# A matrix inverse by doubling: block transposes on VectorE, and narrow tiles for the upper levels

## The reference

```python
lower = jnp.where(strict, jnp.einsum('bhncd,bhnsd->bhncs', kb, k) * decay, 0.0)
tinv = lax.linalg.triangular_solve(lower + eye, eye, left_side=True, lower=True, unit_diagonal=True)
u = jnp.einsum('bhncs,bhnsv->bhncv', tinv, v * beta)
w = jnp.einsum('bhncs,bhnsd->bhncd', tinv, kb * jnp.exp(g))
```

## Time and profile before

| | us |
|---|---|
| median of 3 runs | 1895.49 (1892.24 to 1897.36) |
| the profiled execution, its time | 1895.78 |
| its span, first to last instruction | 1893.8 |
| PE busy | 1811.6 (96%) |
| DVE busy | 1004.5 (53%) |
| ACT busy | 645.8 (34%) |
| POOL busy | 558.5 (29%) |

### The profile page before, as it was taken

One profiled execution on the slowest core, in us unless ns is written; L12 is line 12 of the kernel. 1 busy time (PEld: TensorE's weight loads), 2 busy tenths in 40 slices (PEclk: granted clock), 3 DMA queues, 4 the chain that ended last, 5 costly groups with the idle time before them and its releaser, 6 DMA issues.

```text
span 1893.8 us, 29921 instructions
## 1 busy us (share of the span) xinstructions
PE 1811.6 (96%) x11609; PEld 1743.1 (92%) x11609; DVE 1004.5 (53%) x971; ACT 645.8 (34%) x1028; POOL 558.5 (29%) x492
## 2 busy tenths in 40 slices
PE   5999999987999999999996999999999999999997
PEld 5999999987999999999996989899999999999996
DVE  4477777762445445535545055645554554454556
ACT  6443333354344344335333253221222112122123
POOL 2344555423442333333240211121222212213120
PEclk9999999998999999999998999999999999999999
DMA  6132332323232422422338411111111111111112
GB/s 180 48 95 86 90 91 86 87 107 115 69 92 73 114 61 59 113 61 71 104 95 252 156 34 34 34 56 44 48 52 43 45 44 55 44 33 55 44 44 89
DMA packets 189848, 146.99 MB, mean 78 GB/s; under 512 B 22940, under 2 KB 178115, under 8 KB 188660
## 3 DMA queue, kind: packets, MB, share of 16 engines
q1 hardware_dynamic: 148740, 114.88, 20.8%
q10 hardware_dynamic: 40848, 31.49, 5.4%
q0 software_dynamic: 224, 0.12, 0.0%
HBM read 109.72 MB, written 36.74 MB: 77 GB/s over the span
## 4 chain that ended last, share of the span: by engine, by line
PE 83%; DVE 5%; issue 5%; DMA 2%; ACT 2%; POOLq 1%; DVEq 1%; POOL 1%; SPq 1%; ACTq 0%
PE gb L707 57%; PE db L970 12%; PE db L812 7%; PE db L809 3%; PE db L748 1%; DMA yo<-ot_d 1%; PE db L849 1%; PE db L848 1%; DVEq L1346 1%; DVE hx L1613 1%; POOLq L653 0%; PE db L923 0%; DVE fino L1719 0%; PE db L720 0%; ACT hx L1016 0%
## 5 line engine op out<-in xcount | busy, mean ns | idle before, releaser
L707 PE MATMUL gb<-u_hi,w_hi 128*128 128x342 f32 (+2 forms) x2520 | 827.1, 328 | 17.6 <-ACT ht L1255 7.3
L707 PE MATMUL gb<-u_lo,w_hi 128*128 128x342 f32 (+2 forms) x2520 | 812.2, 322 | 0.0
L707 PE MATMUL gb<-u_hi,w_lo 128*128 128x342 f32 (+2 forms) x2520 | 809.0, 321 | 0.0
L595 POOL TENSOR_TENSOR w_lo<-w_raw,w_hi 128x1024 fp32r<-128x1024 f32 x128 | 335.8, 2630 | 884.6 <-ACT w_hi L1012 884.6
L707 PEld LDWEIGHTS gb<-u_hi,w_hi 128*128 128x128 f32 x2520 | 479.9, 190 | 19.6 <-issue 18.0
L707 PEld LDWEIGHTS gb<-u_lo,w_hi 128*128 128x128 f32 x2520 | 480.0, 190 | 0.5
L707 PEld LDWEIGHTS gb<-u_hi,w_lo 128*128 128x128 f32 x2520 | 479.1, 190 | 0.0
L1390 DVE SCALAR_TENSOR_TENSOR cacc<-xb,prm,cacc 128x1040 f32<-128x1040 f32 x72 | 174.3, 2421 | 11.2 <-issue 10.5
L1685 DVE TENSOR_TENSOR h<-h,db 128x512 f32<-128x512 f32 x176 | 117.1, 685 | 57.4 <-PE db L970 57.0
L970 PE MATMUL db<-w_hi,a_hi 128*128 128x512 f32 x352 | 140.2, 398 | 3.4 <-DVE a_lo L1709 2.9
L1012 ACT ACTIVATE w_hi<-w_raw 128x1024 fp32r<-128x1024 f32 x128 | 133.6, 1052 | 18.7 <-ACT tm L1077 17.3
(11 more groups left out here) (218 smaller groups left out, 2104.7 us busy)
## 6 DMA issues: line engine op xcount, KB each, us to landing
w_raw<-in_w_in SPq DMA_DIRECT2D x53, 512.0 KB, 3.9
w_raw<-in_w_up SPq DMA_DIRECT2D x44, 512.0 KB, 3.7
qkv_d<-tm ACTq DMA_DIRECT2D x24, 576.0 KB, 3.1
tk<-qkv_d SPq DMA_DIRECT2D x9, 1536.0 KB, 7.7
w_raw<-in_w_down SPq DMA_DIRECT2D x22, 512.0 KB, 3.3
ot_d<-ots ACTq DMA_DIRECT2D x9, 512.0 KB, 3.2
yb_d<-ybs ACTq DMA_DIRECT2D x8, 513.0 KB, 3.8
yl<-yb_d SPq DMA_DIRECT2D x8, 513.0 KB, 5.2
```

The lines of the kernel that those rows point to most:

```text
L595: pool.tensor_tensor(w_lo[:, n % SLOTS, :], w_raw[:, n % SLOTS, :], w_hi[:, n % SLOTS, :].bitcast(F32), ALU.subtract).then_inc(s_wlo, 1)
L707: mm = pe.matmul(gb[:, bank, 0:w], wt, u, start=(k == 0 and m == 0), stop=(k == KT - 1 and m == 2))
```

## The change

- The transposes TT0, T0 and T1 leave PE and ACT. DVE makes rr out of bd, and tt_m out of rr after Y0, by an instruction that transposes each 32x32 block in its place. Both matrices have nothing outside their 32x32 diagonal blocks then.
- Level 32 computes only the tiles that it needs. X1 is two products for each head with 32 weight columns and 32 moving columns; Y1 is three, of which the third makes the lower tile for tt_m. DVE evicts tiles of 32 partitions, two or three instructions for each half.
- Level 64 (the top) is one quarter: X2 and Y2 are products of 64 by 64 columns.
- STEPS has 19 steps. The pieces are dealt out anew: GROW has 1 and not 3, OT 5 and not 2, Y0 2 and not 1, X1 1 and not 0; TT0, T0 and T1 had one each.
- In the projection stage ACT squares the transposed tile out of db, and only for the 16 tiles of q and k. POOL only makes w_lo there. DVE sums only those 16 tiles, and the last sum leaves the pooling part.

```diff
-STEPS = ["P1", "TKN", "V", "TKB", "GROW", "KK", "TQ", "TKG", "O", "SU", "QK", "TQD", "OT", "TT0"]
+STEPS = ["P1", "TKN", "V", "TKB", "GROW", "KK", "TQ", "TKG", "O", "SU", "QK", "TQD", "OT"]
...
-    DOUBLING += [f"X{_n}", f"Y{_n}"] + ([f"T{_n}"] if _n < len(LEVELS) - 1 else [])
+    DOUBLING += [f"X{_n}", f"Y{_n}"]
...
-FILLS = {"P1": 2, "TKN": 0, "V": 1, "TKB": 0, "GROW": 3, "KK": 2, "TQ": 2, "TKG": 2, "O": 2, "SU": 2, "QK": 1,
-         "TQD": 1, "OT": 2, "TT0": 1, "X0": 1, "Y0": 1, "T0": 1, "X1": 0, "Y1": 1, "T1": 1, "X2": 0, "Y2": 1}
+FILLS = {"P1": 2, "TKN": 0, "V": 1, "TKB": 0, "GROW": 1, "KK": 2, "TQ": 2, "TKG": 2, "O": 2, "SU": 2, "QK": 1,
+         "TQD": 1, "OT": 5, "X0": 1, "Y0": 2, "X1": 1, "Y1": 1, "X2": 0, "Y2": 1}
...
@@ gpsimd
-                pool.tensor_tensor(sq[:, :, :], tm[:, :, :], tm[:, :, :], ALU.mult).then_inc(s_sq, 1)
...
@@ tensor
+                elif name == "X1":
+                    def left_squares(o, m):
+                        for z in (0, HALF):
+                            t = pe.matmul(o[z + SQ:z + HALF, 0:SQ], at_m[:, m, z + SQ:z + HALF], tt_m[:, m, z:z + SQ],
+                                          start=True, stop=True)
+                        return t
+                    each([(s_tt, 2 * (c - 1))], left_squares)
+                elif name == "Y1":
+                    def right_squares(o, m):
+                        for z in (0, HALF):
+                            pe.matmul(o[z:z + SQ, 0:SQ], nmx[:, m, z:z + SQ], rr[:, m, z + SQ:z + HALF],
+                                      start=True, stop=True)
+                        return pe.matmul(o[SQ:HALF, 0:SQ], rr[:, m, SQ:HALF], nmx[:, m, 0:SQ], start=True, stop=True)
+                    each([done["X1"], done["Y0"]], right_squares)
+                elif name == TOP_X:
+                    each([done["Y1"]], lambda o, m: pe.matmul(
+                        o[HALF:, 0:HALF], at_m[:, m, HALF:], tt_m[:, m, 0:HALF], start=True, stop=True))
+                elif name == LAST_Y:
+                    each([done[TOP_X]], lambda o, m: pe.matmul(
+                        o[0:HALF, 0:HALF], nmx[:, m, 0:HALF], rr[:, m, HALF:], start=True, stop=True))
...
@@ scalar
+                    if squared:
+                        q = act.activation(sq[:, c0:c1, :].rearrange("p c d -> p (c d)"), db[:, r, 0:(c1 - c0) * P],
+                                           ACT.Square)
...
@@ vector
+            def turned_squares(dst, src):
+                return dve.transpose(dst.rearrange("p m c -> p (m c)"), src.rearrange("p m c -> p (m c)"))
...
+                elif name == "X0":
+                    dve.wait_ge(s_bd, 16 + 16 * BLKS * c)
+                    dve.wait_ge(s_ps["V"], 2 * c)
+                    turned_squares(rr, bd).then_inc(s_rr, 1)
+                    halves(name, c - 1, lambda h: dve.tensor_tensor(
+                        heads(nmx, h), dbank(name, h), over_heads(lvl(0), HEADS // 2), ALU.mult), s_ev[name])
+                elif name == "Y0":
+                    for h in range(2):
+                        dve.wait_ge(s_ps[name], 2 * (c - 1) + h + 1)
+                        dve.tensor_tensor(heads(rr, h), heads(rr, h), dbank(name, h), ALU.subtract).then_inc(s_ev[name], 1)
+                        drain()
+                        turned_squares(heads(tt_m, h), heads(rr, h)).then_inc(s_tt, 1)
+                elif name == "X1":
+                    for h in range(2):
+                        dve.wait_ge(s_ps[name], 2 * (c - 1) + h + 1)
+                        for z in (0, HALF):
+                            t = dve.tensor_copy(heads(nmx, h)[z + SQ:z + HALF, :, z:z + SQ],
+                                                dbank(name, h)[z + SQ:z + HALF, :, 0:SQ])
+                        t.then_inc(s_ev[name], 1)
...
```

More of the change, by code:

```diff
@@ L352, in hybrid_block @@
         s_bd = sem("s_bd")
+        s_rr = sem("s_rr")
+        s_tt = sem("s_tt")
         s_osq = sem("s_osq")
@@ L606, in _ @@
             pool.memset(pb[:, 0:16], 0.0).then_inc(s_zero, 1)
[L608 to L613, removed]
-                pool.tensor_tensor(sq[:, :, :], tm[:, :, :], tm[:, :, :], ALU.mult).then_inc(s_sq, 1)
-            for j in range(3):
-                squares(j)
+            for j in range(2, 5):
+                w_low(W_QKV + j)
             with pool.Fori(0, QKV_TILES // 3 - 1) as i:
-                for j in range(3, 6):
-                    squares(j, i)
+                for j in range(5, 8):
+                    w_low(W_QKV + j, i)
             for n in range(W_QKV + QKV_TILES + 2, W_ZG):
@@ L867, in _ @@
                     step(name, 0, (held[-1], 0) if held else None)
-            step("TT0", 0, (same_banks("TT0", PREP_STEPS)[-1], 0))
             pe.wait_ge(s_ev["QK"], 2)
+            pe.wait_ge(s_ev["TQD"], 2)
             def piece(p, i):
@@ L1102, in _ @@
                 qkv_tile(j)
-            with act.Fori(0, QKV_TILES // 3 - 1) as i:
+            with act.Fori(0, 4) as i:
                 for j in range(3, 6):
                     qkv_tile(j, i)
+            for j in range(15, 18):
+                qkv_tile(j, squared=j <= 2 * HEADS)
+            with act.Fori(0, 2) as i:
+                for j in range(18, 21):
+                    qkv_tile(j, i, False)
             def exponentials():
@@ L1168, in act_step @@
                         act.activation(heads(ex, h), heads(ex, h), ACT.Exp).then_inc(s_dec, 1)
-                elif name == "TT0":
-                    copy_halves(name, rr, c - 1, turns=c)
-                elif name in DOUBLING and name[0] == "T":
-                    copy_halves(name, tt_m, c - 1)
                 elif name == "V":
@@ L1194, in _ @@
                     act_step(name, 0)
-            for h in range(2):
-                act.wait_ge(s_ps["TT0"], h + 1)
-                act.activation(heads(rr, h), dbank("TT0", h), ACT.Copy).then_inc(s_ev[LAST_Y], 1)
             def gates(u, i):
@@ L1400, in _ @@
             conv(0, 0)
-            with dve.Fori(0, QKV_TILES // 3 - 1) as i:
+            with dve.Fori(0, 5) as i:
                 for j in range(3):
@@ L1404, in _ @@
                     sums(3 * i + j)
-            for n in (QKV_TILES - 2, QKV_TILES - 1):
-                conv(n, n % 3)
-                sums(n - 1)
+            conv(16, 16 % 3)
+            sums(15)
+            with dve.Fori(0, 2) as i:
+                for j in range(3):
+                    conv(17 + 3 * i + j, (17 + j) % 3)
+            conv(QKV_TILES - 1, (QKV_TILES - 1) % 3)
             def by_chunk(m):
@@ L1473, in _ @@
                 if q == 0:
-                    sums(QKV_TILES - 1)
                     cumulate()
```

63 lines of the change are left out of this document (38 added, 25 removed).

## The result

The changed kernel takes 1844.14 us (median of 4 runs, 1842.80 to 1847.27), against 1896.42 for the kernel before beside it (4 runs, 1892.24 to 1898.61). The ratio is 0.9729, with a 95% interval of 0.9707 to 0.9751. The profiled execution has 1845.04 us at a span of 1843.2, which is 50.6 less than before.

What follows compares the result with a forecast made beforehand. PE, busy 96% of the span, was taken to bound the kernel. Eight loop rounds saving 19.3 us plus 2.2 before the loop made 21.5, so 1895.8 - 21.5 = 1874.3 us, range 1850 to 1887.

Steps and rivals of the forecast that it cites:

- the price of a narrow instruction: Loop, X1 and Y1: each 32-column fp32 matmul instruction costs PE 0.0625 us, taken from a run of 16-column transposes.
- The two steps: Loop, X1 and Y1 on PE: 2.17 and 3.17 us a round, the pair growing from 3.79 to 5.34.
- the sum: Loop on PE: 10.19 us removed less 2.17 + 3.17 + 2.44 put back, saving 2.41 a round, 19.3 in eight.
- that row: Profile row of 18 transposes of 16 columns near 361 us, starting 0.0625 us apart; price source for narrow products.
- The fast rival: Loop's narrow products: instructions paced by their columns, 0.028 us each, 22 us more saved, 1852.2 us; chance 0.21.
- The slow rival: Loop, X1 and Y1: a narrow instruction costs a wide one's 0.112 us, 31.7 us more, 1906.0 us; chance 0.08.
- The drain rival: Loop: PE empties at each change of tile, 0.15 us each, six a round, 7.1 in all, 1881.4 us; chance 0.09.
- X2 and Y2: Loop's top level: 2.44 us in place of 3.79, at 0.0625 a start, saving 1.35 a round despite a 0.27 wait.
- What leaves PE: Loop: TT0, T0 and T1 (2.61 us) and wide X1+Y1 and X2+Y2 (3.79 each) removed, 10.19 a round.
- DVE's transposes: Loop: costed at nothing, 0.68 us for a tt_m half, 1.4 for rr with masks, both covered by PE's work.
- bd and TQ: Loop: bd loads gain about 1.5 us of slack; less cover for TQ's scaling, some tenths may show.
- Projection and bridge: Before the loop: ACT's squares cost nothing; freed DVE adds and last sum gain 2.2 us, not 5.1, capped by PE.

Runs made afterwards that it cites:

- e3: Changed kernel with X1's and Y1's narrow products issued tile by tile, so neighbours use the same column tile; 1851.23 us, ratio 0.9765.
- e4: Changed kernel with X1's products given all 128 weight columns at 32 moving columns; 1874.74 us, ratio 0.9895.
- e5: Changed kernel with level 32 computed by whole products again, Y1's third product staying narrow; 1883.38 us, ratio 0.9929.
- e6: Changed kernel with X2 and Y2 each split into two products of 32 weight and 64 moving columns; 1843.39 us, ratio 0.9719.
- e8: Changed kernel with DVE's transposition of each half into tt_m made twice; 1853.72 us, ratio 0.9773.
- e7: Changed kernel with level 16 narrow too: X0 and Y0 as four products for each head, DVE subtracting in four tiles; 1838.05 us, ratio 0.9694.
- e2: Kernel before the change with squares on ACT for all 24 tiles and all 24 sums kept on DVE; 1894.35 us, ratio 0.9991.
- e1: Kernel before the change with only the projection part of the change, old loop; 1894.85 us, ratio 0.9992.
- e12: Changed kernel without the projection part, so only the loop part of the change; 1848.72 us, ratio 0.9751.
- e9: Changed kernel with X1's products given all 128 moving columns at 32 weight columns; 1853.76 us, ratio 0.9781.

## Why the prediction was wrong, step by step

- **The step that failed** is the price of a narrow instruction: "I take 0.0625, since among the narrow instructions of the trace it is the nearest in kind". It was 0.016 in X1 and 0.011 in Y1. The step left out that two or three column tiles work side by side, and its price was twice the 0.030 that one tile takes (e3). The two steps cost 0.81 + 0.83 = 1.64, where the sum had 2.17 + 3.17 = 5.34: 3.70 a round, 29.6 in eight. The forecast was off by 30.2 (1874.3 - 1844.1).
- **Why that row misled.** It was a run of small transposes, 16*128 16x16: 16 moving columns, but 128 weight columns. e4 shows that with 128 weight columns an fp32 instruction on 128 rows costs 0.109 even when only 32 move. The row's form showed both numbers; the rival named the weight columns, and the sum went by the moving ones. Why the row itself costs 0.0625 and not 0.109 stays open: it has 16 rows where e4 has 128, and it is a transpose; but a transpose of the loop, with 128 rows and columns, costs 0.87 / 8 = 0.109 too. The Trainium skill's two floors, about 62 and about 25 ns ("TensorE: Matmul & The Clock Gate", section "Wait — 56ns, not 53.3ns?"), don't hold here: starts lie 0.016, 0.011 and 0.009 us apart, below both, so that the row's 62.5 ns agreed with the first of them says nothing about narrow products.
- **The fast rival** ("paced by their columns", 1852.2, chance 0.21) was right in kind and too small. Its 0.028 is a quarter of 0.112 in one tile, where 0.030 was measured (e3); what it lacked was the overlap of the column tiles (0.016 with two in turn, 0.011 with three, 0.009 with four). 80 x 0.028 = 2.24 a round against 1.04 measured for the 80 starts; 1.2 x 8 = 9.6 us. One of its reasons was no reason: at 11 us the transposes of 16 columns are 0.105 apart, but so soon after the start those of 128 columns are slow as well, 0.22 apart (12.68 us, eight in 1.97) against 0.109 in the loop.
- **The slow rival** (0.112 an instruction) is what e4 made of X1, with 128 weight columns. With 32 nothing speaks for it.
- **The drain rival** had the right price, in e5 above all (0.15 a change; 0.15 to 0.16 measured), but 0.17 a narrow step was in the sum already, and the two changes of a step cost 0.3. The term was 0.13 too small for each of X1 and Y1, some 2 us in all, in the other direction.
- **X2 and Y2**: 2.44 predicted, 2.52 measured; 0.0625 a start predicted, 0.060 to 0.062 measured; the gap of 0.3 as predicted. That the value was right is luck: it is half of 0.112 and a little more, the price of 64 columns, and no floor, as the 0.028 a start of e6 shows.
- **What leaves PE**: TT0, T0, T1 and the wide products, 10.19. With the measured 4.16 taken off it gives 6.03 against the measured 5.98, so the sum's first half was right.
- **DVE's transposes**: 0.71 and 1.23, predicted 0.68 and 1.4. PE never waited for them in the changed kernel, but with 0.4 us left where 1.2 were computed; e8 and e7 made that wait appear.
- **bd and TQ**: no wait of PE for bd inside the loop, and for TKN's form 0.7 a round as before; no wait for TQ.
- **Projection and bridge**: 354 us with PE busy for 351.8, so ACT's squares cost nothing, as predicted. All adds at 1.24, and the last sum was covered (e2). 2.2 predicted, 2.5 in the timelines; the run times give 1.5 (e1) to 4.6 (e12). The 2.2 was PE's idle time up to the product; counted between starts PE was 2.3 late (376.06 - 373.58 - 0.16), and the copy came 0.75 after the product's start, 0.59 in the changed kernel.

## What to carry to other kernels

Read the whole form of a row before taking its price for an instruction that the trace lacks, and vary one number of the form at a time; here the price went with the larger of weight and moving columns, and both have to be small. Narrow products pay most when neighbours in the queue go to different column tiles and when whole and narrow products don't take turns. After a step on the critical engine has become shorter, recount the cover of each neighbour's work: the same narrowing at level 16 brought 0.5 us a round with the pieces where they were and 1.9 with one moved.

## What the runs showed of the hardware that was not expected

The price of an fp32 instruction of TensorE by its columns, with 128 rows, from the starts in these runs:

| weight x moving columns | column tiles in turn | us a start | times the tiles | from |
|---|---|---|---|---|
| 128 x 128 | 1 | 0.112 | 0.112 | |
| 128 x 32 | 1 | 0.109 | 0.109 | e4 |
| 64 x 64 | 1 | 0.060 to 0.062 | the same | changed |
| 32 x 128 | 2 | 0.054 to 0.059 | 0.108 to 0.118 | e9 |
| 32 x 64 | 2 | 0.028 | 0.056 | e6 |
| 32 x 32 | 1 | 0.030 | 0.030 | e3, end of Y1 |
| 32 x 32 | 2 | 0.016 | 0.032 | changed, X1 |
| 32 x 32 | 3 | 0.011 | 0.033 | changed, Y1 |
| 32 x 32 | 4 | 0.009 | 0.036 | e7 |

In e4 the granted clock fell for a few us at the end of X1. The windows of e4, second round, X1 ending at 566.5:

```profile
562.00:564.00 2.00, 2.00 (x19) 2.00 (x18) 0.45 (x1) 0.46 (x1) 0.00 (x0) 1.00 0.00 0
564.00:566.00 2.00, 2.00 (x20) 2.00 (x19) 0.58 (x2) 0.00 (x0) 0.00 (x0) 0.97 0.00 0
566.00:570.00 4.00, 4.00 (x61) 3.59 (x61) 0.84 (x3) 0.00 (x0) 0.00 (x0) 0.59 0.00 0
```

PE was busy without a break, with 32 instructions of 128 weight and 32 moving columns for some 3.7 us; then the clock was at its lower level (1.2 GHz) for most of the 4 us. This came in five of the eight rounds. Four of them took 65.6 to 67.1 from V to V; the three without a dip took 64.14 to 64.18, 2.75 more than in the changed kernel. The fifth is the last round, shorter in every kernel, with 4.25 more than there. So e4's 30.6 us are 22 of X1's price and the rest of the clock. The granted clock of every other kernel's loop was 1.00. What sets the dip off was not tried further.

POOL's work slowed DVE. The four taps' three fused instructions have the mean below in the changed kernel (groups of DVE by form):

```profile
L1406 DVE SCALAR_TENSOR_TENSOR cacc<-xb,prm,cacc 128x1040 f32<-128x1040 f32 x72 | 109.0, 1514 | 11.3 <-issue 10.6
```

In e12, with the squares back on POOL, it is this:

```profile
L1403 DVE SCALAR_TENSOR_TENSOR cacc<-xb,prm,cacc 128x1040 f32<-128x1040 f32 x72 | 174.3, 2420 | 11.2 <-issue 10.5
```

In e2, with the squares on ACT but all sums on DVE, the mean is 1329 ns, so the sums aren't the cause. The timelines of DVE and of POOL in the kernel before show which of the taps are slow:

```profile
299.46 1.30 DVE L1390 SCALAR_TENSOR_TENSOR cacc<-xb,prm,cacc 128x1040 f32<-128x1040 f32 x1 [0.17 <-issue]
300.93 2.90 DVE L1390 SCALAR_TENSOR_TENSOR cacc<-xb,prm,cacc 128x1040 f32<-128x1040 f32 x1 [0.17 <-issue]
303.99 3.19 DVE L1390 SCALAR_TENSOR_TENSOR cacc<-xb,prm,cacc 128x1040 f32<-128x1040 f32 x1 [0.17 <-issue]
...
299.78 2.95 POOL L614 TENSOR_TENSOR sq<-tm 128x1152 f32<-128x1152 f32 x1 [6.12 <-ACT tm L1077]
302.69 3.39 POOL L595 TENSOR_TENSOR w_lo<-w_raw,w_hi 128x1024 fp32r<-128x1024 f32 x1
```

A tap that starts while POOL works on a square or on a weight subtraction (w_lo) takes 2.9 to 3.3 us and ends 1.1 us after that instruction; one that starts before POOL does, or while POOL is idle, takes 1.30. This holds for all 72 in the kernel before (23 start in a square, 23 in a subtraction) and for all 72 in the changed kernel, where 8 start in a subtraction. The adds of the earlier trace rows go the same way: the one at 361.90 starts 0.04 before the square and takes 1.24, the next two start inside POOL's work. So it is not the square as such; moving the squares to ACT also took the subtractions from under the taps. That is 65 us of DVE's time in the projection stage, all of it hidden behind PE.
